# The third matrix of each expert loaded as rows 2p and 2p+1 per partition, in pieces of 8192 bytes

## What is computed

```python
h1 = jnp.einsum('td,edf->tef', t, p['w1'])
h3 = jnp.einsum('td,edf->tef', t, p['w3'])
hh = jax.nn.silu(h1) * h3 * gate[:, :, None].astype(t.dtype)
return jnp.einsum('tef,efd->td', hh, p['w2']).reshape(bn, n, d)
```

## Time and profile before

| | |
|---|---|
| median of 3 runs | 1041.42 us (1034.93 to 1042.8) |
| profiled execution, time | 1039.06 us |
| its span, mean granted TensorE clock | 1037.2 us, 0.961 |
| TensorE, VectorE, ScalarE, GpSimd busy | 919.0, 399.1, 238.6, 120.2 us |
| bytes moved by DMA | 318.82 MB, 307 GB/s over the span |
| packets of SyncE's queue | 53472, 285.84 MB |
| packets of GpSimd's queue | 13328, 25.02 MB |

### The profile page before, as it was taken

One profiled execution on the slowest core, in us unless ns is written; L12 is line 12 of the kernel. 1 busy time (PEld: TensorE's weight loads), 2 busy tenths in 40 slices (PEclk: granted clock), 3 DMA queues, 4 the chain that ended last, 5 costly groups with the idle time before them and its releaser, 6 DMA issues.

```text
span 1037.2 us, 14352 instructions
## 1 busy us (share of the span) xinstructions
PE 919.0 (89%) x5439; PEld 515.1 (50%) x5439; DVE 399.1 (38%) x1155; ACT 238.6 (23%) x598; POOL 120.2 (12%) x131
## 2 busy tenths in 40 slices
PE   4899879998899998988889987998879999889880
PEld 1345436546555554555456553554565555545450
DVE  2103277235622252311263565663563222522114
ACT  3101134211111111111344454432111111111111
POOL 1000000100122221121100000001001222212110
PEclk9899989998999999999999998999999999999896
DMA  9969799358699999998860048008798999999964
GB/s 378 398 275 389 294 421 415 119 197 269 251 413 413 407 407 410 397 414 364 302 238 9 1 165 297 36 1 290 265 398 325 415 416 411 415 384 414 414 281 188
DMA packets 69011, 318.82 MB, mean 307 GB/s; under 512 B 12502, under 2 KB 13526, under 8 KB 46536
## 3 DMA queue, kind: packets, MB, share of 16 engines
q1 hardware_dynamic: 53472, 285.84, 69.3%
q0 software_dynamic: 13328, 25.02, 7.0%
q10 hardware_dynamic: 2144, 7.05, 1.7%
HBM read 312.72 MB, written 26.49 MB: 327 GB/s over the span
## 4 chain that ended last, share of the span: by engine, by line
PE 64%; DMA 19%; DVE 10%; ACT 2%; issue 2%; SPq 1%; POOL 0%; POOLq 0%; DVEq 0%; ACTq 0%
PE psum L797 16%; DMA ring<-in_l_w 12%; PE psum L810 8%; PE psum L993 7%; PE psum L747 4%; DMA ring<-in_l_w_ada 3%; PE psum L1210 3%; PE psum L1108 2%; PE psum L1099 2%; PE psum L777 2%; PE psum L633 2%; PE psum L1140 2%; PE psum L768 2%; DMA scratch<-token_rows_hbm,overflow_rows 2%; PE psum L760 1%
## 5 line engine op out<-in xcount | busy, mean ns | idle before, releaser
L797 PE MATMUL psum<-ring,scratch 128*64 128x256 f32 x1792 | 215.0, 394 | 19.7 <-DMA ring<-in_l_w 18.1
L797 PEld LDWEIGHTS psum<-ring,scratch 128*64 128x64 f32 x1792 | 134.8, 141 | 85.7 <-issue 34.2
L1988 DVE TENSOR_TENSOR scratch<-scratch,psum 64x256 f32<-64x256 f32 x64 | 27.2, 424 | 301.0 <-ACT scratch L1358 296.6
L810 PE MATMUL psum<-ring,scratch 128*64 128x512 f32 x464 | 112.2, 604 | 2.6 <-ACT scratch L1362 1.9
L2445 POOL DMA_INDIRECT expert_rows<-scratch,slot_rows x64 | 63.4, 990 | 339.1 <-ACT scratch L1372 339.1
L1358 ACT ACTIVATE scratch<-psum 64x256 f32<-64x256 f32 x64 | 24.0, 375 | 257.1 <-PE psum L797 250.7
L993 PE MATMUL psum<-ring,scratch 128*128 128x512 f32 x192 | 75.3, 552 | 1.3 <-DVE scratch L2121 1.3
L1372 ACT COPY scratch<-psum 128x512 f32<-128x512 f32 x64 | 37.5, 585 | 147.4 <-PE psum L810 147.4
L633 PE MATMUL psum<-ring,scT 128*32 128x512 f32 x320 | 42.9, 660 | 16.9 <-DMA ring<-in_l_w_ada 15.8
L993 PEld LDWEIGHTS psum<-ring,scratch 128*128 128x128 f32 x192 | 36.9, 195 | 38.1 <-issue 37.0
L810 PEld LDWEIGHTS psum<-ring,scratch 128*64 128x64 f32 x464 | 29.2, 136 | 42.2 <-issue 37.2
(11 more groups left out here) (343 smaller groups left out, 1205.4 us busy)
## 6 DMA issues: line engine op xcount, KB each, us to landing
ring<-in_l_w SPq DMA_DIRECT2D x168, 1024.0 KB
ring<-in_l_w_ada SPq DMA_DIRECT2D x48, 1024.0 KB, 4.8
ring<-in_l_w_o SPq DMA_DIRECT2D x8, 1024.0 KB
ring<-in_l_w_in SPq DMA_DIRECT2D x4, 1024.0 KB
gate_rows<-gate_rows_hbm POOLq DMA_DIRECT2D x8, 512.0 KB, 7.7
scale_shift<-gate_rows_hbm POOLq DMA_DIRECT2D x8, 512.0 KB, 10.4
gate_rows<-in_l_w SPq DMA_DIRECT2D x4, 1024.0 KB
scale_shift<-in_l_w SPq DMA_DIRECT2D x4, 1024.0 KB
```

The lines of the kernel that those rows point to most:

```text
L797: last = nc.tensor.matmul(ps[64 * n:64 * n + 64, 2 + par, 0:DE], mine[:, k, :], part(w, k * DE, DE), start=k == 0, stop=k == KD - 1)
L810: last = nc.tensor.matmul(ps[64 * n:64 * n + 64, 5 + par, :], hhT[:, par, k, :], part(w2, k * D + n * 512, 512), start=k == 0, stop=k == 1)
```

## The change

`load_matrix` loads w2 so that partition p holds rows 2p and 2p+1, which are neighbours in memory: one run of 8192 bytes. In this form the two parts of the matrix in the partition are the even and the odd rows. So VectorE writes the even columns of the product to columns 0 to 127 of `hh` and the odd ones to 128 to 255, for the 32 experts and the overflow block. It reads both inputs in straight order and writes with a distance of 128 elements between neighbours.

```diff
--- before.py
+++ after.py
@@ -307,6 +307,7 @@
         rows = view(W, 3072, 2, NT, 2 * SLOTS)
         silu = W[64:128, 4480:4736]
         hh = W[:, 4736:4992]
+        hh_by_part = hh[64:128, :].rearrange("p (k j) -> p j k", k=2)
         hhT = view(W, 5120, 2, 2, SLOTS)
         ysb = view(W, 5376, 2, 512)
 
@@ -449,8 +450,8 @@
                     src = w[bass.ds(e, 1)].rearrange("e (p k) f -> p (e k f)", k=KD)
                     dst = tile
                 else:
-                    src = w[bass.ds(e, 1)].rearrange("e (k p) d -> p (e k) d", p=P)
-                    dst = tile.rearrange("p (k d) -> p k d", k=2)
+                    src = w[bass.ds(e, 1)].rearrange("e (p k) d -> p (e k d)", k=2)
+                    dst = tile
                 return sp.dma_start(dst, src)
 
             def load_expert(l, e, g, n):
@@ -1985,7 +1986,8 @@
 
                 def product(e, u):
                     dve.wait_ge(S["silu_ready"], e + (base + 1))
-                    V.tensor_tensor(hh[64:128, :], silu, ps[64:128, 2 + u % 2, 0:DE], ALU.mult)\
+                    V.tensor_tensor(hh_by_part, silu.rearrange("p (j k) -> p j k", k=2),
+                                    ps[64:128, 2 + u % 2, 0:DE].rearrange("p (j k) -> p j k", k=2), ALU.mult)\
                         .then_inc(S["hh_ready"], 1)
 
                 def ahead(e, j, u):
@@ -2065,7 +2067,8 @@
                                              ps[:, half, :].rearrange("p (k s) -> p k s", s=P)[:, :, 0:SLOTS])
                     last.then_inc(S[f"ov_dve_steps{l}"], 1)
                     dve.wait_ge(S[f"ov_act_steps{l}"], b * 3 + 1)
-                    V.tensor_tensor(hh[64:128, :], silu, ps[64:128, 2, 0:DE], ALU.mult).then_inc(S[f"ov_dve_steps{l}"], 1)
+                    V.tensor_tensor(hh_by_part, silu.rearrange("p (j k) -> p j k", k=2),
+                                    ps[64:128, 2, 0:DE].rearrange("p (j k) -> p j k", k=2), ALU.mult).then_inc(S[f"ov_dve_steps{l}"], 1)
 
                     dve.wait_ge(S[f"ov_pe_steps{l}"], b * 5 + 5)
                     dve.sem_inc(S[f"ov_free{l}"], 1)
```

## The result

The changed kernel takes **1046.66 us** (median of 20 runs, 1039.19 to 1054.2) against 1041.2 us of the kernel before (20 runs beside it); the ratio is 1.0054, with a 95% interval of 1.0035 to 1.0073. The forecast was 1043 us: the sign was right. Its terms gave +3.6 us on the profiled execution, and the number lay only 1.6 us above the median then known, since that execution was 2.4 us under it; the measured loss is 5.5 us. The profiled execution took 1044.67 us, its span is 1042.8 us at a mean granted clock of 0.954, against 1037.2 us at 0.961 before.

The account below looks back on a forecast made before the run. TensorE sets the pace until step 18, back-to-back matrix loads after overflow. Layer 0 +2.3 us and layer 1 +1.3 us, together +3.6 us on the profiled 1039.06 us, gave 1042.7, forecast 1043 us; range 1034 to 1049 us.

Parts of the forecast that it names:

- the sign: Whole kernel: the change makes it slower, +3.6 us by the terms.
- turns by packet: Shared engines: each software-queue packet waits for about one SyncE packet, whose mean grows from 220 to 304 ns.
- The first rival: Larger packets of one queue don't hold up the other; -2.4 us in all, 1036.6 us; chance 0.26.
- The gather before step 17: Expert stage, each layer: gathered token rows land 2.0 us later, all exposed as TensorE wait.
- full alternation: Gather before step 17: all 36 software packets per engine wait 84 ns more, landing 3.1 us later; two thirds taken.
- The overflow gather: Before the overflow block: 19 packets per engine wait longer, 1.0 us per layer, at most 1.6 us.
- the third rival: Expert stages: all packets alternate and TensorE returns at half clock after longer gather waits; +12.2 us, 1051 us; chance 0.09.
- The second part: From overflow to the last landing: eight third matrices save 0.10 us each, -0.8 us per layer.
- The product: VectorE's product goes from 0.42 to about 0.60 us; on the path at step 0 and overflow, +0.36 us per layer.
- Between the layers: Stretch between the experts of the two layers: +0.2 us only.
- the terms: Without gather delays: pieces save 0.8 us per layer in the second part, the product costs 0.36 us per layer.

Follow-up runs that it names:

- e2: Changed kernel, but layer 1 writes its product in straight order and keeps the 8192-byte pieces; 1047.86 us, ratio 1.005.
- e1: Changed kernel, but layer 1 loads its third matrices in two 4096-byte pieces as before and keeps the split-column product; 1044.59 us, ratio 1.0039.
- e11: Changed kernel with third matrices loaded in two 4096-byte pieces in both layers, split-column product kept; 1040.75 us, ratio 0.999.
- e9: Kernel before, plus a half-size gate-row spread ahead of step 14's gather and another ahead of the overflow gather, both layers; 1047.02 us, ratio 1.0057.
- e3: Kernel before, but layer 1's first and second matrices also come in two 4096-byte pieces per partition; 1043.14 us, ratio 1.0016.
- e4: Changed kernel with the two gate-row spreads issued one step later, behind step 14's scatter; 1039.05 us, ratio 0.9961.
- e6: Changed kernel with gate-row spreads one step later and the overflow gather ahead of the ordinary one; 1038.72 us, ratio 0.9965.
- e7: Kernel before with gate-row spreads one step later and the overflow gather ahead of the ordinary one; 1043.61 us, ratio 1.0007.
- e10: Changed kernel with gate-row spreads one step later and the product written in straight order in both layers; 1038.10 us, ratio 0.9956.
- e8: Kernel before with the gate-row spreads issued one step later; 1042.50 us, ratio 0.9986.

## Why the prediction was right, and where it was off

**What bounds the kernel, and turns by packet.** Right. The pieces alone bring the waits (e2), the product alone doesn't (e1, e11), and packets stay one for one (234 to 238, then 218 to 223) while SyncE's grow from 242 to 296 ns. The first rival, turns that cost nothing, is out.

**The gather before step 17.** Forecast +2.0 us in each layer; the waits grew by 1.64 us in layer 0 and 1.96 in layer 1. Of the 3.1 us that full alternation would give, that is between a half and two thirds; I had taken two thirds.

**The overflow gather.** Forecast +1.0 us by its own longer transfer; that is 0.75 us in both layers (8.70 and 8.89 us from issue to landing, 7.95 and 8.14 before). The wait in layer 0 grew by 1.98 us all the same, for a reason that the prediction had not worked out. The gather is issued behind step 17's scatter, so it inherits the whole delay of step 17 (issue at 400.83 instead of 397.46, 3.37 us later), while TensorE makes a part of the delay good, because the matrix waits of steps 18 and 19 vanish, 1.4 us in all. The sum for the stretch: 3.37 later, plus 0.75, less the 0.46 us by which the layer began later, is 3.66 us, the difference of the table. That sum is 1 us over the forecast 2.7, and 1.64 us of it are half clock at 385.59 and 386.92 (1.40 for 1.09, 3.27 for 1.94).

**The step that failed: half clock.** It stood as the third rival, at 0.09, with the condition that all packets alternate and the wait reaches 4.3 us, which "has to pass the 2.02 us after which, at 479.89, the matmuls still took 3.67". The forecast's own wait of 1.2 + 2.0 us passes 2.02 as well, and it came at 2.84 to 3.43 us, so half clock belonged to the forecast and not to a rival. And 2.02 us was no bound, by the trace of the kernel before itself: the wait of 2.15 us that the earlier trace rows show at 268.86 is followed by 5.36 us for 3.67, and so are waits of 2.16 us (463.46), 2.00 us (495.36, 5.30 us) and 1.83 us (777.18). One row at full clock was taken for a limit. The kernel before:

```profile
269.22 5.36 PE L797 MATMUL psum<-ring,scratch 128*64 128x256 f32 x32
463.46 5.36 PE L797 MATMUL psum<-ring,scratch 128*64 128x256 f32 x32 [2.16 <-DMA ring<-in_l_w]
```

In the expert stages half clock costs, from the rows of the changed kernel, 0.31 + 1.33 + 0.45 + 2.38 = 4.5 us in layer 0 and 0.88 + 0.63 + 0.88 + 1.55 = 3.9 us in layer 1. The rival had priced the clock at 2.6 us per layer, too little, and yet its sum of +12.2 us was too much. By the table the two expert stages lost 0.8 us in all, less than the forecast's 3.2, so nearly all of these 8.4 us was given back. Two causes can be read: the stretches behind overflow lie beside the matrices that TensorE would otherwise wait for, and layer 1 of the kernel before had begun with half clock itself (its second up-projection at 777.54 took 5.36 us, after the change 3.67).

**The second part.** Forecast -0.8 us per layer from the pieces. The parts became 1.8 and 2.2 us shorter, and the matrix waits in them fell to 3.6 and 4.4 us, far more than "somewhat below 8.0 and 6.6 us". Of the time, 1.2 and 1.1 us come from lateness alone, by e9's profile. With the 0.18 us of the product put back, 0.8 and 1.3 us are left for 8 third matrices, 0.10 to 0.16 us each; e3 gives 0.06 us. So the forecast 0.10 us (12 ns for two pieces) lies inside what single profiles give.

**The product.** 610 ns for 600, +0.2 us at each of four places, nothing elsewhere. Right in each point.

**Between the layers.** Forecast nothing but 0.2 us; the profiled executions differ by 4.0 us. The waits there are alike (5.3 and 5.8 us for the conditioning matrices, and for VectorE no line differs by more than 0.5 us); the granted clock is 0.95 instead of 0.96, and of the 4.0 us 3.2 are one step of the attention's length, with half clock behind waits that are equally long in both (1.81 and 1.72 us). This stretch has the largest scatter of all: 282.4 us in e11, 285.3 in e4, 287.8 in e6 and in e7, 290.8 in e10 whose only gather wait is one of 0.95 us, 292.6 in e9. So from one profile its 4.0 us can't be put down to the waits. The longer attention doesn't need long gather waits either: it is two steps longer in e10, and one in e4, e6, e7 and e8. Over all runs the kernels with four long waits do have the lowest clock (the table above), and that is as far as it goes. Whether and by what path a wait in one layer's experts would change the clock 100 us later is open, and no run here was made for it.

**What stays open besides.** Once the gathers are out of the way, the change is worth 3.1 us (1.0 to 5.1), or 2.6 us (0.5 to 4.8) with each kernel taken against its own runs of before, where the terms say 1.6 - 0.7 = 0.9 us. The second interval holds this, so the terms are neither confirmed nor refuted; a part of the difference may be clock again (0.9585 and 0.9586 against 0.9581 and 0.9573).

**The number.** The mechanism (late gathers by packet turns) and the places of the waits were right; mis-sized were the clock (zero in the sum) and what the second part gives back (0.8 for 1.8 and 2.2 us). The two errors were of opposite sign, which kept 1046.66 within 4 us of 1043. That is luck in part: the profiled executions put the loss mainly between the layers, where the forecast had nothing, and the way there is not shown.

## What to carry to other kernels

Before pieces of a busy queue are made larger, look at who shares the engines with it: here a small transfer behind many packets of its own queue waited for about one packet of the other queue per turn, and longer when those were larger. Put bulk transfers of the slow queue behind the gathers that somebody waits for, and only then enlarge the pieces; here the same change makes the kernel 0.5% slower in one order, and 0.4% faster than it was in the other. And look up every wait of the profile together with the time of the matmuls behind it, not one row: where a wait grows to a length after which half clock is seen, price these matmuls at half clock in the forecast itself.

## What the runs showed of the hardware

- From run to run, time and TensorE's granted clock go together in this kernel: 0.74 us for 0.001 over 99 runs (correlation -0.87), with times from 1034 to 1052 us. One stretch without any change, the attention of layer 1, took about 207.5, 211 or 214.4 us in 13 traces.
- After the gather waits of 2.84 to 3.43 us TensorE ran at 1.2 GHz for a while, beginning at once or up to some 2 us later. The length of one wait does not settle it: up-projections took 5.36 us after 1.80 (980.50 in e10) and 2.18 us (907.69 in e4), 5.30 after 2.00 (495.36 before), but 3.67 us after 2.00 (493.00 in e7), 2.02 and even 3.29 us (986.56 in e8).
- Two pieces of 4096 bytes took 8 to 20 ns more than one of 8192 (8 ns by e3; 0.10 and 0.16 us for 8 pairs by the second parts of the changed kernel and e9; one profile each).
- A VectorE product of 256 columns that writes with a hop of 512 bytes took 610 ns instead of 424, 0.73 ns more per element; the line that the earlier trace rows show gave 0.70.
